# Two pairs of small products of one left factor, each issued as one product over two right factors, in the chunked delta rule of a trunk kernel

## What is computed

```
def step(s, inp):
    r_t, w_t, k_t, v_t, z_t, bb_t = inp
    sz = jnp.einsum("bhij,bhj->bhi", s, z_t)
    s = s * w_t[:, :, None, :] + sz[..., None] * bb_t[:, :, None, :] + v_t[..., None] * k_t[:, :, None, :]
    return s, jnp.einsum("bhij,bhj->bhi", s, r_t)
...
_, y = lax.scan(step, s0, (tm(r_h), tm(w_h), tm(k_h), tm(v_h), tm(z_h), tm(b_h)))
```

## Time and profile before

| | us |
|---|---|
| median of 3 runs | 1491.04 |
| lowest, highest | 1490.84, 1494.11 |
| the profiled execution: its time | 1490.77 |
| the profiled execution: its span | 1489.0 |
| PE matmul busy in the span | 1444.4 (97%) |
| mean granted clock of PE | 0.987 |

### The profile page before, as it was taken

One profiled execution on the slowest core, in us unless ns is written; L12 is line 12 of the kernel. 1 busy time (PEld: TensorE's weight loads), 2 busy tenths in 40 slices (PEclk: granted clock), 3 DMA queues, 4 the chain that ended last, 5 costly groups with the idle time before them and its releaser, 6 DMA issues.

```text
span 1489.0 us, 21859 instructions
## 1 busy us (share of the span) xinstructions
PE 1444.4 (97%) x9700; PEld 1191.5 (80%) x9700; DVE 830.7 (56%) x1039; ACT 509.8 (34%) x590; POOL 73.2 (5%) x67
## 2 busy tenths in 40 slices
PE   6999999998999999998999999999998999999997
PEld 5777777777888888887888888888887888888886
DVE  7768676767635354444746454455437645354455
ACT  7455454533312222223344332322424313122222
POOL 1000000013000000001200000000013000000000
PEclk9999999998999999999999999999998999999999
DMA  4111111102323222231222122123121322223221
GB/s 183 73 36 58 50 58 34 69 30 74 138 86 113 85 98 100 87 112 62 83 83 85 57 91 108 57 89 110 57 85 50 134 85 90 109 85 113 85 98 72
DMA packets 19726, 125.54 MB, mean 84 GB/s; under 512 B 2288, under 2 KB 2288, under 8 KB 5808
## 3 DMA queue, kind: packets, MB, share of 16 engines
q1 hardware_dynamic: 19088, 121.23, 22.7%
q0 software_dynamic: 544, 2.91, 0.6%
HBM read 122.03 MB, written 2.10 MB: 83 GB/s over the span
## 4 chain that ended last, share of the span: by engine, by line
PE 91%; DVE 4%; ACT 2%; issue 1%; POOL 1%; DMA 1%; SPq 0%; DVEq 0%; ACTq 0%; POOLq 0%
PE bank L339 20%; PE bank L345 20%; PE bank L342 20%; PE bank L543 4%; PE bank L540 4%; PE bank L544 4%; PE bank L1473 2%; PE bank L1476 2%; PE bank L1470 2%; PE bank L783 2%; PE bank L353 2%; PE bank L790 1%; PE bank L1506 1%; PE bank L1505 1%; PE bank L1504 1%
## 5 line engine op out<-in xcount | busy, mean ns | idle before, releaser
L339 PE MATMUL bank<-XH,WH 128*128 128x512 f32 x944 | 380.4, 403 | 24.3 <-DVE XL L432 12.6
L345 PE MATMUL bank<-XH,WL 128*128 128x512 f32 x944 | 371.6, 394 | 0.0
L342 PE MATMUL bank<-XL,WH 128*128 128x512 f32 x944 | 371.6, 394 | 0.0
L312 DVE TENSOR_TENSOR WL<-raw,WH 128x2048 fp32r<-128x2048 f32 (+1 forms) x111 | 249.7, 2251 | 174.3 <-ACT WH L306 174.2
L306 ACT ACTIVATE WH<-raw 128x2048 fp32r<-128x2048 f32 (+1 forms) x111 | 208.1, 1877 | 277.9 <-DMA raw<-weights 277.9
L339 PEld LDWEIGHTS bank<-XH,WH 128*128 128x128 f32 x944 | 180.0, 191 | 66.5 <-issue 28.3
L342 PEld LDWEIGHTS bank<-XL,WH 128*128 128x128 f32 x944 | 180.1, 191 | 38.4 <-issue 2.4
L345 PEld LDWEIGHTS bank<-XH,WL 128*128 128x128 f32 x944 | 179.6, 190 | 38.6
L656 ACT ACTIVATE AH<-relu 128x512 fp32r<-128x512 f32 x64 | 40.5, 633 | 250.0 <-DVE relu L681 250.0
L681 DVE SCALAR_TENSOR_TENSOR relu<-bank,rB 128x512 f32<-128x512 f32 x64 | 44.2, 690 | 100.0 <-PE bank L345 100.0
L339 PE MATMUL bank<-AH,WH 128*128 128x512 f32 x256 | 99.7, 389 | 0.0
(11 more groups left out here) (327 smaller groups left out, 2025.3 us busy)
## 6 DMA issues: line engine op xcount, KB each, us to landing
raw<-weights SPq DMA_DIRECT2D x107, 1024.0 KB, 4.8
raw<-weights SPq DMA_DIRECT2D x8, 512.0 KB, 4.8
h<-x_fm SPq DMA_DIRECT2D x4, 512.0 KB, 8.1
out_tm<-hT SPq DMA_DIRECT2D x8, 256.0 KB, 2.1
rc<-ret_const POOLq DMA_DIRECT2D x1, 1536.0 KB, 6.7
pp<-pairs POOLq DMA_DIRECT2D x4, 199.0 KB, 4.3
cst<-const SPq DMA_DIRECT2D x1, 577.0 KB, 12.0
gain_row<-last_gain POOLq DMA_DIRECT2D x1, 512.0 KB, 3.6
```

What stands on the lines that cost most here:

```text
L312: nc.vector.tensor_tensor(WL[i][:, :n], raw[i][:, :n], WH[i][:, :n], ALU.subtract).then_inc(S("w_lo"), 1)
L339: mm = pe.matmul(bank[b][:], wh, xh, start=(k == 0), stop=False)
L342: mm = pe.matmul(bank[b][:], wh, xl, start=False, stop=False)
L345: mm = pe.matmul(bank[b][:], wl, xh, start=False, stop=(k == len(xs) - 1))
```

## The change

The factors W[0] and W[1] get one buffer `w_pair`, and Bt and lax one buffer `b_a`. "w1" and "w2" become one `two_turned` product "w" into twin 3, "gg" and "qq" one product "gq" into twin 2. Both copies that "w1" and "w2" needed are now waited for ahead of "w". ACT copies the first half of twin 3 (`w1_s`), and DVE copies the second half (`w2_s`) once `w1_s` is done. `g_s` and `q_s` read the two halves of twin 2.

```
-            need("t1z_s", "ip2")
-            turned(pe, 2, W[8], W[0], "w1")
-            need("t1x_s")
-            turned(pe, 3, W[8], W[1], "w2")
+            need("t1z_s", "t1x_s", "ip2")
+            two_turned(pe, 3, W[8], w_pair, "w")
             between(5)
             need("w1_s", "b_by_token")
-            turned(pe, 1, W[7], Bt, "gg")
-            turned(pe, 2, W[7], lax, "qq")
+            two_turned(pe, 2, W[7], b_a, "gq")
             need("w2_s", "k_by_token")
...
-            evac("w1", W[7], 2, "w1_s")
+            evac("w", W[7], 3, "w1_s")
...
-            copied(W[9], 3, "w2", "w2_s")
-            unit_added(W[11], 1, "gg", "g_s")
-            need("qq", "rd_ready")
-            nc.vector.tensor_tensor(blocks(W[10]), by_parity(Rd), blocks_of_twin(2), ALU.add).then_inc(S("q_s"), 1)
+            need("w1_s")
+            nc.vector.tensor_copy(halves(W[9]), of_twin(3, 1)).then_inc(S("w2_s"), 1)
+            unit_added(W[11], 2, "gq", "g_s")
+            need("rd_ready")
+            nc.vector.tensor_tensor(blocks(W[10]), by_parity(Rd), blocks_of_twin(2, 1), ALU.add).then_inc(S("q_s"), 1)
```

More of the change, by code:

```diff
@@ L78 @@
     "chunk_products": "azb azb_t azb_n m2 m2_t z_turned m4 e2 azk_t m8 e4 v_turned e8 x2 po po_t yz k_turned po2 t1z t1x "
-                      "b_turned w1 w2 gg qq",
+                      "b_turned w gq",
     "low_rank_factors": "decay_rate iclr g_out",
@@ L201, in trunk_kernel @@
         ab = Place()
-        W = [ab(f"W{i}", T) if i not in (4, 5, 10) else None for i in range(12)]
+        W = [ab(f"W{i}", T) if i not in (0, 1, 4, 5, 10) else None for i in range(12)]
         unit_squared, z_r, z_x = ab("unit_squared", [2, T]), ab("z_r", [2, T]), ab("z_x", [2, T])
+        w_pair, b_a = ab("w_pair", [2, T]), ab("b_a", [2, T])
         W[4], W[10] = unit_squared[:, 0, :], unit_squared[:, 1, :]
+        W[0], W[1] = w_pair[:, 0, :], w_pair[:, 1, :]
+        Bt, lax = b_a[:, 0, :], b_a[:, 1, :]
         W[5], Rd = z_r[:, 0, :], z_r[:, 1, :]
@@ L210, in trunk_kernel @@
         yH, yL = ([ab(f"{n}{i}", [2, T], F32R) for i in range(2)] for n in ("yH", "yL"))
-        Bt, Kt, Vt, ARB, ARK, O = (ab(n, T) for n in ("Bt", "Kt", "Vt", "ARB", "ARK", "O"))
+        Kt, Vt, ARB, ARK, O = (ab(n, T) for n in ("Kt", "Vt", "ARB", "ARK", "O"))
         bonus, gout, mixdiff = (ab(n, T) for n in ("bonus", "gout", "mixdiff"))
-        lora, gate_in, lax, Uag = (ab(n, T) for n in ("lora", "gate_in", "lax", "Uag"))
+        lora, gate_in, Uag = (ab(n, T) for n in ("lora", "gate_in", "Uag"))
         Ur, Uk, Uv, Uax = (ab(n, T + w) for n, w in (("Ur", 1), ("Uk", 1), ("Uv", 1), ("Uax", 3)))
```

## The result

| | before | after |
|---|---|---|
| median of 20 runs, us | 1492.25 | 1497.13 |
| lowest, highest | 1490.84, 1497.52 | 1492.61, 1504.45 |
| ratio | | 1.0032 (95%: 1.0021 to 1.0043) |
| the profiled execution: time, span | 1490.77, 1489.0 | 1496.24, 1494.4 |

The change made the kernel slower, by about 4.9 us. I had said 1493.5, and 1496.6 was the top of the range.

What follows compares the result with a forecast made beforehand. It took a chain with no slack (product, copy, product, three DVE operations, loop) to bound the chunk products; 0.98 + 0.99 + 2 x 0.26 = 2.49 us on 1491.04 gave 1493.5, range 1490.4 to 1496.6.

Steps and rivals of the forecast that it cites:

- The chain: Products and copies ahead of the chunk loop, all four pairs: loops start later by 2.49 us together; chance 0.64.
- the other three terms: Later chunk-loop starts in pair 3 (0.99 us) and in pairs 1 and 2 (0.26 us each).
- The signs named ahead: Pair 0 after: 64x128 records from 79.30, PE idle some 0.9 us ahead of "gq", loop at about 83.8, not 82.84.
- the fillers of pairs 1 and 2: Three large matmuls between "w2" and "gg" there give the chain's first half 0.6 us of slack.
- a saving on PE: At each of eight places one doubled product takes 0.99 us instead of 1.09, saving 0.10 us.
- `w2_s` at nothing: DVE's added copy in pair 0 ends 0.43 us before `g_s` can start, so it costs nothing.
- The delay passed on in full: Any later start of a pair's chunk loop delays everything behind it equally; nothing behind absorbs it.
- The clock: Rival: new PE idle time in pairs 0 and 3 lowers the clock; 1496.9 us for one stretch, 1500.2 for two; chance 0.06.
- The pauses that move: Rival: 512 fewer PE records shift unexplained pauses costing 1.8 us in pair 3; chance 0.12 gone or fewer, 0.08 more.
- the two cases: Pair 3's pauses go, giving 1491.7 us (gone or fewer 0.12), or pair 0 gets them too, giving 1495.3 (more 0.08).

Runs made afterwards that it cites:

- pad_pe: Kernel before with eleven products of pair 0 made twice, so later PE instructions stand 44 places further on; 1496.09 us, ratio 1.0001.
- delay_each1: Kernel before with one more unread DVE copy ahead of `g_s` in each pair; 1497.00 us, ratio 1.0031; run again: 1497.40 us, 1.0044.
- layout: Kernel before with the change's side-by-side buffers but its own four products; 1494.38 us, ratio 1.0007.
- warm_tails: Kernel before with unread matmuls between layer parts: one of 256 columns behind the sums, four of 512 behind the spread of roots; 1495.92 us, ratio 1.0012.
- after_busy: Changed kernel with one unread 128x128 by 128x320 matmul between "w" and "gq" in pairs 0 and 3; 1496.55 us, ratio 1.0022.
- after_busy2: Changed kernel with unread 64x64 matmuls: eight ahead of "gq" in pairs 0 and 3, three ahead of the `g_s` wait in all pairs; 1492.31 us, ratio 0.9998.

## Why the prediction was wrong

- **The chain: right.** "In pair 0: 0.26 ... + 0.36 ... + 0.36 ... = 0.98" and the other three terms make 2.49 us; the two traces show 2.83, the fit at the same clock 2.39 +- 0.30. The signs named ahead were there: 64x128 records, idle PE ahead of "gq" (0.71 us, 0.9 forecast), and the fillers of pairs 1 and 2 covering the first half. The mis-sized parts are small: 0.05 us a link, and a saving on PE of 0.05 us a place where 0.10 had been put.
- **`w2_s` at nothing: right.** It starts at 81.28 in pair 0 and DVE is idle 0.50 us behind it.
- **The delay passed on in full: right.** The kernel with one unread copy a pair starts its loops 0.60 + 0.59 + 0.60 + 0.48 = 2.27 us later in the trace and loses 2.37 us at the same clock, with no product changed.
- **The clock: the step that failed.** I took a fall as a rival of 0.06, as one event inside the pairs that happens or doesn't, and put it at nothing in the sum and outside the range. I read the place from one trace, where the clock stood at 1.00 around the change. But low runs came to 26 of 66 with the change and to 29 of 154 without it, and that is worth 1.2 us on the mean, 1.9 in the 20 runs of the comparison. It is a shift in how often runs are low, and it should have stood in the sum as a term.
- **Why it looked safe: a reading of the rows that was wrong.** The forecast puts the 0.50 near 338 "after the long idle stretch" and sets against it the pause of 0.73 us, which took no clock. The trace has it the other way round: the clock fell at about 335 us and the long idle time came after.
```profile
334.00:338.00 4.00, 3.43 (x22) 3.35 (x22) 2.47 (x2) 1.48 (x2) 0.00 (x0) 0.64 0.00 0
```
```profile
343.18 0.77 PE L339 MATMUL bank<-XH,WH 128*128 128x512 f32 x1 [4.21 <-DVE XL L432]
```

Ahead of the fall PE had been idle for 1.44 us, until 333.46, and had then made matmuls of one column. So the rows held no fall behind a long idle time with which the forecast's 0.9 us could be compared. The price was off too: 3.3 us for one stretch was read from a window of 10 us, and the two stretches in the midst of large matmuls cost 1.57 and 1.38.

- **The base.** I started from 1491.04, a median of three; with twenty it is 1492.25. That is 1.2 of the 3.6 us by which I missed, and it is the luck of three runs. With the clock's 1.9 it is 3.1; the last 0.5 is open (the means of the 20 and 20 runs lie 4.91 apart, the medians 4.88). Neither the clock nor the base alone would have passed the 1496.6: 1493.5 + 1.9 is 1495.4.
- **The pauses that move: right as a mechanism, wrong in what sets them off.** In pair 3 they got shorter by about 0.2 to 1.4 us, over the four pairs together by some 0.2 on the mean, so neither of the two cases (all gone, or as many in pair 0) came. I had bound them to the density of small instructions; pad_pe shows that the place in the program matters.

## What to carry to other kernels

Two products merged into one save only the time between them (0.05 us here) and make the first consumer wait for both (0.41 us here): merge where nobody waits for the first half. A short stall of PE in front of a latency-bound loop (one whose steps wait for each other) can cost more than its length, because low-clock runs can get more frequent, 10 of 21 in delay_each1; price it with the scatter of many runs and not with one profile, and look at the mean clock of each run beside its time. A change of under 3 us can be drowned by the pauses in PE's stream, which a few added or removed instructions can move.

## What the runs showed of the hardware that was not expected

- After 2.62 us of idle PE the clock went to 0.50 and stayed there through a loop of 64x64 products in which PE was busy for 3.83 + 3.88 of 8 us, until large matmuls had run for a while.
- The clock also fell where PE was hardly idle: at 367 us in the kernel after, behind 16 matmuls of one column and in the midst of large ones. The same code showed it in four of six traces of the kernel after, and in layout, pad_pe and delay_each1, which have the products of before, and not in the trace of before. What decides is open.
- In the kernel before the clock fell at about 335 us behind only 1.44 us of idle PE and matmuls of one column, ahead of the 4.21 us of idle time and not behind it.
- Extra matmuls raise the mean clock (0.990 in warm_tails) without lowering the time (1.0012): the mean clock alone isn't a measure of a kernel.
- Open stays where the clock falls in the low runs of the changed kernel, and why after_busy didn't help where after_busy2 did.
